# Down slots of three dense feed forwards as three single-pass products, their remainders on GpSimd

## The chip, the cores and the metric

One NeuronCore of a Trainium2 chip runs the kernel. The metric is the device time of one execution in microseconds.

## What is computed

Two two-layer blocks behind each other on a sequence of 256 tokens of width 1024, batch 1, all float32. The plan of four layers is `first0`, `first1`, `even`, `odd`. Each layer is a mixer, an output product and a feed forward, each with a norm and a modulation. Three of the four feed forwards are dense; `first1` has a mixture of 8 experts. Cut to what matters:

```python
def swiglu(x, w1, w3, w2):                       # first0
    return (jax.nn.silu(x @ w1) * (x @ w3)) @ w2

def conv_ffn(h, w_up, conv_w, conv_b, w_down):   # even, odd
    gate, val = jnp.split(h @ w_up, 2, axis=-1)
    gate = causal_dwconv(gate, conv_w) + conv_b  # 3 taps
    return (jax.nn.silu(gate) * val) @ w_down

mod = cond @ w_ada[layer] + b_ada[layer]         # 6 x 1024 numbers for each layer
```

with `D_FF = 2816`. The change touches the dense products with `w2` and `w_down`.

## The kernel before

Weights stream from HBM in slots of 128 x 2048 floats (1 MB) through a ring of six (`ring`, RING = 6), loaded by SP in the order in which TensorE uses them; a place in the ring is loaded anew when the semaphore `weights_used` says that the slot six places earlier has been used. A dense feed forward is 11 chunks of 256 hidden columns. A chunk c has three slots: two for up (w = 0 and 1) and one for down. TensorE's order is up(0), then up(c+1), down(c) for c = 0 to 9, then down(10). Chunks 0, 1 and 10 are written out, 2 to 9 are a loop of two chunks per turn (`each_chunk`); the other engines call `visit(c, odd)` in the same order.

A product can be made in two ways. `mm` on float32 data takes four passes. The other way (`mm3`) takes a number apart into a part rounded to float32r and the remainder, and sums three products of a single pass: high x high, high x low and low x high. The up slots of chunks 1 to 10 are made so: ACT copies the slot from `ring` to one of four buffers `w_high` (`high`, L1095), which rounds it; GpSimd subtracts this from the slot in place (`low`, L732), which leaves the remainder in `ring_rounded`, the same memory; TensorE waits for it on `split_low`. In the same way `h_high` (L1099) and `h_low` (L725) are made once per feed forward. up(0) and all down slots are made with four passes, straight from `ring` and from `ff_hid`.

For chunk c ACT's visit is: the loads of a group of modulation weights (below), rounding of up(c+1), w = 0 (`high(c, odd, 0)`), silu of both halves of chunk c (L1134, or L1128 after the convolution), rounding of up(c+1), w = 1. DVE's visit: in `even` and `odd` the convolution from PSUM into `ff_mid` (L1805, L1808), then two products with silu into `ff_hid` (L1802), and, for chunks 2 to 9 of `first0` and `even`, a group of the next layer's modulation (`mod_parts`): three slots of 128 x 2048, each in two dots of 1024 columns (`dot`, L1814, SCALAR_TENSOR_TENSOR with an accumulator). ACT loads the three slots of a group (L813) only when `mod_part` counts all dots of the group before. `odd` is the last layer and has no such dots. GpSimd has nothing else in these stretches than L725 and L732.

```python
load_modulation(n + 1, c - 2)          # ACT: waits mod_part of the group before
...
pool.wait_ge(split_high, q + (before + 1))   # GpSimd, L731
pool.tensor_tensor(ring_r[:, at, :], ring[:, at, :], f32(w_high[r]), ALU.subtract)
```

## Time and profile before

| | us |
|---|---|
| median of 3 runs | 2631.04 (2624.57 to 2635.58) |
| the profiled execution's own time | 2632.19 |
| its span, first to last instruction | 2630.4 |
| PE busy | 2494.7 (95%) |
| DVE busy | 1773.1 (67%) |
| ACT busy | 1199.3 (46%) |
| POOL busy | 332.0 (13%) |

PE is TensorE, PEld its weight loads, DVE VectorE, ACT ScalarE, POOL GpSimd. A row of a timeline gives the start in us from the start of the span, the duration, the engine, the line and the instruction, output<-inputs, how many are merged (x3), and in brackets the idle time before with what ended it. An instruction that waits for a memory port counts as busy. A matmul in four passes stands as two records, and ends of matmuls are modelled.

### The profile page before, as it was taken

To read this page: it belongs to the slowest core of one execution; us is meant where nothing else is said; L and a number is where in the kernel's file an instruction comes from. 1 tells how busy PE (TensorE), PEld (TensorE's weight loads), DVE (VectorE), ACT (ScalarE), POOL (GpSimd) and SP (SyncE) were. 2 spreads that over 40 slices of the span, in tenths; PEclk is the share of its full clock that TensorE was granted. 3 is DMA by queue.
4 is the path that set the end of the run, shared out by engine and by line. 5 is a ranking of instruction groups with operands and counts; after the bars stand their busy time and mean duration, and the time that the engine had idled before them with its cause. 6 is when DMAs were issued, how large, how long until landed. Compare 5 with 4: busy or idle time off the path is not lost.

```text
span 2630.4 us, 36293 instructions
## 1 busy us (share of the span) xinstructions
PE 2494.7 (95%) x13972; PEld 2157.5 (82%) x13972; DVE 1773.1 (67%) x1949; ACT 1199.3 (46%) x1273; POOL 332.0 (13%) x97
## 2 busy tenths in 40 slices
PE   4999999989999999999999998899999899988999
PEld 3888997877888888888888886788999788977998
DVE  5832775768888888888888886374389777751222
ACT  3213213117676767666666665222321456642221
POOL 0005541000000000000000000010455000001542
PEclk8989999999999999999999999899999999988999
DMA  8845874766999999999999998121588343322542
GB/s 343 320 150 208 347 317 168 288 240 257 349 336 343 342 340 341 342 342 342 340 343 340 341 343 318 65 96 65 202 335 321 124 145 131 142 96 80 172 165 95
DMA packets 90380, 656.13 MB, mean 249 GB/s; under 512 B 10032, under 2 KB 10288, under 8 KB 10800
## 3 DMA queue, kind: packets, MB, share of 16 engines
q1 hardware_dynamic: 80928, 589.34, 59.9%
q10 hardware_dynamic: 9360, 65.52, 6.2%
q8 instruction: 64, 1.05, 0.2%
q14 instruction: 28, 0.23, 0.0%
HBM read 653.76 MB, written 1.05 MB: 249 GB/s over the span
## 4 chain that ended last, share of the span: by engine, by line
PE 71%; issue 17%; POOL 6%; DVE 2%; ACT 2%; DMA 2%; ACTq 0%; POOLq 0%; DVEq 0%
PE bank L1158 70%; POOL ring_rounded L732 6%; DMA consts<-consts_dram 1%; PE bank L1663 1%; DVE rstd L1862 0%; ACT ff_mid L1060 0%; DVE xT L1808 0%; DMA ring<-stream_dram 0%; ACT ff_silu L1059 0%; ACT work_rounded L773 0%; PE bank L1514 0%; DVE work L1808 0%; DVE work L2375 0%; DVE yT L1808 0%; DVE ring L1814 0%
## 5 line engine op out<-in xcount | busy, mean ns | idle before, releaser
L1802 DVE TENSOR_TENSOR ring_rounded<-ring,work_rounded 128x2048 fp32r<-128x2048 f32 x372 | 842.2, 2290 | 142.0 <-ACT work_rounded L907 121.7
L1158 PE MATMUL bank<-work_rounded,proj_rounded 128*128 128x512 f32 x1792 | 614.2, 406 | 2.4 <-DVE proj_rounded L1802 2.0
L907 ACT ACTIVATE work_rounded<-ring 128x2048 fp32r<-128x2048 f32 x224 | 428.3, 1913 | 0.0
L1158 PEld LDWEIGHTS bank<-work_rounded,proj_rounded 128*128 128x128 f32 x1792 | 338.0, 189 | 78.7 <-issue 3.0
L1158 PE MATMUL bank<-ring_rounded,proj_rounded 128*128 128x512 f32 x896 | 353.4, 394 | 0.0
L1158 PE MATMUL bank<-work_rounded,ff_hid_rounded 128*128 128x512 f32 x896 | 302.2, 398 | 1.8 <-DVE ff_hid_rounded L1802 1.8
L1158 PE MATMUL bank<-yT_rounded,ring_rounded 128*128 128x256 f32 x960 | 271.6, 283 | 0.0
L1158 PE MATMUL bank<-hT,ring 128*128 128x256 f32 x1088 | 250.7, 392 | 10.4 <-ACT hT L797 10.4
L1158 PEld LDWEIGHTS bank<-hT,ring 128*128 128x128 f32 x1088 | 213.3, 197 | 48.9 <-issue 18.8
L1158 PE MATMUL bank<-ff_hid,ring 128*128 128x256 f32 x1056 | 232.9, 379 | 0.0
L1158 PEld LDWEIGHTS bank<-ff_hid,ring 128*128 128x128 f32 x1056 | 198.4, 190 | 25.9
L914 ACT ACTIVATE work_rounded<-ring 128x2048 fp32r<-128x2048 f32 x112 | 214.2, 1913 | 0.0
L1158 PEld LDWEIGHTS bank<-work_rounded,ff_hid_rounded 128*128 128x128 f32 x896 | 170.2, 190 | 42.8 <-DVE ring_rounded L1802 2.0
L1158 PEld LDWEIGHTS bank<-ring_rounded,proj_rounded 128*128 128x128 f32 x896 | 170.5, 190 | 36.6
L1158 PEld LDWEIGHTS bank<-yT_rounded,ring_rounded 128*128 128x128 f32 x960 | 184.1, 192 | 0.0
L1158 PE MATMUL bank<-ring_rounded,ff_hid_rounded 128*128 128x512 f32 x448 | 178.6, 399 | 0.0
L705 POOL COPY ff_hid<-proj 128x4 f32<-128x4 f32 (+1 forms) x2 | 0.7, 363 | 1286.5 <-ACT proj L820 1286.5
L732 POOL TENSOR_TENSOR ring_rounded<-ring,proj_rounded 128x2048 fp32r<-128x2048 f32 x30 | 144.4, 4823 | 135.4 <-ACT proj_rounded L1095 135.4
L930 ACT ACTIVATE ff_hid_rounded<-bank 128x256 fp32r<-128x256 f32 x112 | 43.1, 385 | 254.4 <-PE bank L1663 243.0
L732 POOL TENSOR_TENSOR ring_rounded<-ring,work_rounded 128x2048 fp32r<-128x2048 f32 x30 | 143.4, 4794 | 114.6 <-ACT work_rounded L1095 114.6
L1805 DVE TENSOR_SCALAR ff_mid<-bank,params 128x256 f32<-128x256 f32 x44 | 23.9, 543 | 194.5 <-PE bank L1158 194.5
L1158 PE MATMUL bank<-yT_rounded,proj_rounded 128*128 128x256 f32 x480 | 138.2, 288 | 2.6 <-POOL ring_rounded L732 2.6
(286 smaller groups left out, 4264.5 us busy)
## 6 DMA issues: line engine op xcount, KB each, us to landing
ring<-stream_dram SPq DMA_DIRECT2D x561, 1024.0 KB, 4.8
work<-stream_dram ACTq DMA_DIRECT2D x56, 1024.0 KB, 9.2
params<-params_dram ACTq DMA_DIRECT2D x1, 1728.5 KB, 28.9
consts<-consts_dram ACTq DMA_DIRECT2D x1, 1568.0 KB, 37.7
cond<-cond_dram ACTq DMA_DIRECT2D x2, 512.0 KB, 3.8
xT<-x_dram ACTq DMA_DIRECT2D x1, 1024.0 KB, 10.0
out_dram<-xT SPq DMA_DIRECT2D x1, 1024.0 KB, 3.9
consts<-consts_dram ACTq DMA_DIRECT2D x1, 577.0 KB, 32.3
```

What stands on the lines that cost most here:

```text
L705: pool.tensor_copy(d[:, j:4, 0:lag], src[:, j:4, 0:lag])
L732: pool.tensor_tensor(ring_r[:, at, :], ring[:, at, :], f32(w_high[r]), ALU.subtract)\
L907: act.activation(up_high[u][half], ring[:, (moe_first + s + half) % RING, :], ACT.Copy)\
L914: act.activation(down_high[u], ring[:, (moe_first + s) % RING, :], ACT.Copy)\
L930: act.activation(ff_hid_r[:, u, :], bank(4 + u, 0, T), ACT.Copy).then_inc(m["hid_t"], 1)
L1158: return pe.matmul(o, lhsT=a, rhs=b, start=start, stop=stop, skip_group_check=True)
L1663: last = pe.transpose(bank(4 + u, j * P, j * P + P), ff_mid[:, u, j * P:j * P + P], const("ident"))
L1802: return dve.tensor_tensor(o, a, b, op)
L1805: return dve.tensor_scalar(o, a, s1, s2, op0, op1)
```

## The change

The third slot of a chunk is now taken apart like the first two.

- ACT: at the end of a visit it waits for `ffn_hid` of the chunk, copies both halves of `ff_hid` to `ff_hid_high` (128 x 512, rounded), and rounds the down slot of the chunk into one of two buffers `ff_down_high`. For the last chunk this is the only rounding of the visit.
- GpSimd: 31 remainders for each dense feed forward instead of 20; a loop turn has six, one more stands behind the loop.
- DVE: a subtraction (`leave_low`, 128 x 512) leaves `ff_hid_low`. In chunks with modulation it stands behind the first of the three slots.
- TensorE: down(c) is 48 products of one pass instead of 16 in four, and waits for `split_low` and `hid_low`.
- `ff_hid_high` and `ff_hid_low` lie in `h_heads`; `cond` is moved behind it, so that the rounded names keep the same addresses as the plain ones. Before the mixer of `first1` GpSimd's memsets now wait until the first feed forward is done, since its buffers lie in the same memory.

```diff
--- before.py
+++ after.py
@@ -198,12 +198,12 @@
         proj = sb("proj", shapes["proj"])
         ff_hid = sb("ff_hid", shapes["ff_hid"])
         work = sb("work", shapes["work"])
-        cond = sb("cond", [P, D])
         ring_r, yT_r, ff_hid_r, work_r = (rounded[name] for name in ("ring", "yT", "ff_hid", "work"))
         pflat = proj[:, :, :, :].rearrange("p a b t -> p (a b t)")
         pflat_r = rounded["proj"][:, :, :, :].rearrange("p a b t -> p (a b t)")
         hT = sb("hT", shapes["hT"])
         h_heads = sb("h_heads", shapes["h_heads"])
+        cond = sb("cond", [P, D])
         xT = sb("xT", [P, KD, T])
         consts = sb("consts", [P, const_n])
         params = sb("params", [P, param_n])
@@ -364,7 +364,10 @@
         w_high = [work_r[:, 0:SLOT], work_r[:, SLOT:2 * SLOT], pflat_r[:, 0:SLOT], pflat_r[:, 2 * SLOT:3 * SLOT]]
         h_high = yT_r
         h_low = pflat_r[:, SLOT:2 * SLOT].rearrange("p (k t) -> p k t", k=KD)
-        assert mod_at >= 2 * SLOT
+        ff_down_high = [work_r[:, mod_at + (MOD_GROUP + u) * SLOT:mod_at + (MOD_GROUP + 1 + u) * SLOT] for u in range(2)]
+        assert mod_at >= 2 * SLOT and mod_at + (MOD_GROUP + 2) * SLOT <= work_n - D
+        ff_hid_high, ff_hid_low = (rounded["h_heads"][:, a * 4 * T:(a + 1) * 4 * T].rearrange("p (b t) -> p b t", b=4)
+                                   for a in range(2))
 
 
         weights_here = [sem(f"weights_here{i}") for i in range(RING)]
@@ -391,6 +394,7 @@
         low_pool = steps("low_pool", "h")
         split_high = sem("split_high")
         split_low = sem("split_low")
+        hid_high, hid_low = sem("hid_high"), sem("hid_low")
         ffn_mid = sem("ffn_mid")
         ffn_silu = sem("ffn_silu")
         ffn_hid = sem("ffn_hid")
@@ -488,8 +492,9 @@
             return ap.bitcast(F32)
 
 
-        SPLITS = 2 * (DENSE_CHUNKS - 1)
-        PAIR_SPLITS = 4
+        SPLITS = 3 * (DENSE_CHUNKS - 1) + 1
+        PAIR_SPLITS = 6
+        split_buffers = [w_high[0], w_high[1], ff_down_high[0], w_high[2], w_high[3], ff_down_high[1]]
         dense_before = [sum(k != "first1" for k in plan[:n]) for n in range(len(plan))]
 
         def each_chunk(eng, chunks, visit):
@@ -677,6 +682,8 @@
 
                 if n:
                     pool.wait_ge(mod_part, parts_before(n + 1))
+                    pool.wait_ge(weights_used, place[f"in{n}"])
+                    pool.wait_ge(split_low, dense_before[n] * SPLITS)
                 else:
                     pool.wait_ge(mod_part, KD)
 
@@ -725,16 +732,17 @@
                 pool.tensor_tensor(h_low, hT[:, :, :], f32(h_high[:, :, :]), ALU.subtract)\
                     .then_inc(*low_pool.step("h"))
 
-                def low(r, q):
-
-                    at = (first + r // 2 * 3 + r % 2) % RING
+                def low(r, q, high):
+
+                    at = (first + r) % RING
                     pool.wait_ge(split_high, q + (before + 1))
-                    pool.tensor_tensor(ring_r[:, at, :], ring[:, at, :], f32(w_high[r]), ALU.subtract)\
+                    pool.tensor_tensor(ring_r[:, at, :], ring[:, at, :], f32(high), ALU.subtract)\
                         .then_inc(split_low, 1)
 
                 with pool.Fori(0, SPLITS // PAIR_SPLITS) as i:
                     for r in range(PAIR_SPLITS):
-                        low(r, i * PAIR_SPLITS + r)
+                        low(r, i * PAIR_SPLITS + r, split_buffers[r])
+                low(0, SPLITS - 1, ff_down_high[0])
 
             for n, kind in enumerate(plan):
                 if kind.startswith("first"):
@@ -1081,9 +1089,9 @@
             def feed_forward(n, kind):
                 base, first = tiles_before[n], place[f"ffn{n}"]
 
-                def high(c, odd, w):
-
-                    at = 3 * odd + w + 2
+                def high(c, odd, w, final=False):
+
+                    at = 3 * odd + (0 if final else w) + 2
                     rounds = (first + at) // RING + 1
                     if isinstance(c, int):
                         act.wait_ge(weights_here[(first + at) % RING], 16 * (rounds + (c - odd) // 2))
@@ -1092,7 +1100,7 @@
                     else:
                         act.wait_ge(weights_here[(first + at) % RING], (c - odd) * 8 + 16 * rounds)
                         act.wait_ge(weights_used, c * 3 + (first + w - 3))
-                    act.activation(w_high[2 * odd + w], ring[:, (first + at) % RING, :], ACT.Copy)\
+                    act.activation(split_buffers[3 * odd + w], ring[:, (first + at) % RING, :], ACT.Copy)\
                        .then_inc(split_high, 1)
 
                 act.wait_ge(*shift_act.at("h7", 2 * n + 1))
@@ -1114,6 +1122,12 @@
                     tiles(c, odd)
                     if not (isinstance(c, int) and c == 0) and not final:
                         high(c, odd, 1)
+                    act.wait_ge(ffn_hid, base + 2 * c + 2)
+                    if not isinstance(c, int) or c >= 2:
+                        act.wait_ge(weights_used, c * 3 + (first - 1))
+                    act.activation(ff_hid_high[:, 2 * odd:2 * odd + 2, :], ff_hid[:, 2 * odd:2 * odd + 2, :], ACT.Copy)\
+                       .then_inc(hid_high, 1)
+                    high(c, odd, 2, final)
                     if n == 0 and final:
                         condition(cond[:, :])
 
@@ -1708,9 +1722,10 @@
 
                 def split_here(c, w, i):
 
-                    q = splits + 2 * (c - 1) + w + 1
+                    r = 3 * (c - 1) + w
+                    q = splits + r + 1
                     pe.wait_ge(split_low, q if i is None else i * PAIR_SPLITS + q)
-                    return w_high[2 * ((c - 1) % 2) + w], ring_r[:, (first + 3 * c - 1 + w) % RING, :]
+                    return split_buffers[r % PAIR_SPLITS], ring_r[:, (first + 2 + r) % RING, :]
 
                 def mm3(o, w, x, start, stop):
 
@@ -1747,18 +1762,20 @@
                         last.then_inc(weights_used, 1)
 
                 def down(c, i=None, final=False):
-                    at = ff_down(first, c, chunks)
-                    arrive(at, i)
-                    w2 = down_k(at)
-                    t = base + 2 * c + 2
-                    pe.wait_ge(ffn_hid, t if i is None else i * 4 + t)
+                    r = SPLITS - 1 if final else 3 * c + 2
+                    q = splits + r + 1
+                    pe.wait_ge(split_low, q if i is None else i * PAIR_SPLITS + q)
+                    parts = [p.rearrange("p (j n) -> p j n", j=2)
+                             for p in (ff_down_high[c % 2], ring_r[:, (first + 2 + r) % RING, :])]
+                    t = dense_before[n] * DENSE_CHUNKS + c + 1
+                    pe.wait_ge(hid_low, t if i is None else i * 2 + t)
                     for j in range(2):
                         b = 2 * (c % 2) + j
                         for d in range(KD):
 
-                            last = mm(bank(d // 2, d % 2 * T, d % 2 * T + T), w2[:, j, d * P:d * P + P],
-                                      ff_hid[:, b, :], i is None and c == 0 and j == 0 and d % 2 == 0,
-                                      final and j == 1)
+                            last = mm3(bank(d // 2, d % 2 * T, d % 2 * T + T), [p[:, j, d * P:d * P + P] for p in parts],
+                                       (ff_hid_high[:, b, :], ff_hid_low[:, b, :]),
+                                       i is None and c == 0 and j == 0 and d % 2 == 0, final and j == 1)
                             if final and j == 1 and d in (1, 3, 5):
                                 last.then_inc(ffn_out, 1)
                     last.then_inc(weights_used, 1)
@@ -2443,14 +2460,24 @@
                                     last.then_inc(ffn_mid, 1)
                             if back < 2:
                                 last.then_inc(ffn_conv, 1)
+                    def leave_low():
+                        dve.wait_ge(hid_high, c + (dense_before[n] * DENSE_CHUNKS + 1))
+                        tt(ff_hid_low[:, 2 * odd:2 * odd + 2, :], ff_hid[:, 2 * odd:2 * odd + 2, :],
+                           f32(ff_hid_high[:, 2 * odd:2 * odd + 2, :]), ALU.subtract).then_inc(hid_low, 1)
+
                     for j in range(2):
                         b = 2 * odd + j
                         dve.wait_ge(ffn_silu, base + 2 * c + j + 1)
                         if late:
                             dve.wait_ge(weights_used, first + 3 * c - 1)
+                            dve.wait_ge(hid_low, c + (dense_before[n] * DENSE_CHUNKS - 1))
                         tt(ff_hid[:, b, :], bank(4 + b, T, 2 * T), ff_silu[:, b, :], ALU.mult).then_inc(ffn_hid, 1)
                     if n + 1 < len(plan) and not isinstance(c, int):
-                        mod_parts(n + 1, c - 2, range(MOD_GROUP))
+                        mod_parts(n + 1, c - 2, range(1))
+                        leave_low()
+                        mod_parts(n + 1, c - 2, range(1, MOD_GROUP))
+                    else:
+                        leave_low()
 
                 each_chunk(dve, chunks, visit)
                 g = mod_columns(n, 5)
```

On GpSimd, the loop of the feed forward of `first0`. Before, one turn and what follows it (L732 is a remainder, L683 the first memset of the next mixer):

```order
L735 ISA
L732 TENSOR_TENSOR ring_rounded<-ring,work_rounded 128x2048 [waits split_high]
L731 REGISTER_ALU
L732 TENSOR_TENSOR ring_rounded<-ring,work_rounded 128x2048 [waits split_high]
L731 REGISTER_ALU
L732 TENSOR_TENSOR ring_rounded<-ring,proj_rounded 128x2048 [waits split_high]
L731 REGISTER_ALU
L732 TENSOR_TENSOR ring_rounded<-ring,proj_rounded 128x2048 [waits split_high]
L735 REGISTER_ALU
L735 COMPARE_AND_BRANCH
L683 MEMSET work 128x1024 [waits mod_part]
```

Now, from the third remainder of a turn on:

```order
L739 TENSOR_TENSOR ring_rounded<-ring,work_rounded 128x2048 [waits split_high]
L738 REGISTER_ALU
L739 TENSOR_TENSOR ring_rounded<-ring,proj_rounded 128x2048 [waits split_high]
L738 REGISTER_ALU
L739 TENSOR_TENSOR ring_rounded<-ring,proj_rounded 128x2048 [waits split_high]
L738 REGISTER_ALU
L739 TENSOR_TENSOR ring_rounded<-ring,work_rounded 128x2048 [waits split_high]
L742 REGISTER_ALU
L742 COMPARE_AND_BRANCH
L739 TENSOR_TENSOR ring_rounded<-ring,work_rounded 128x2048 [waits split_high]
L690 MEMSET work 128x1024 [waits split_low,weights_used,mod_part]
```

A turn of two chunks has six remainders where it had four, the third and the sixth for down slots; a last one stands in front of the memset, whose waits have become three.

On DVE, in a visit of the loop of `first0`, before (L1802 is the product with silu, L1814 the dots):

```order
L1802 TENSOR_TENSOR ff_hid<-bank,ff_silu 128x256 [waits weights_used,ffn_silu]
L1830 ISA
L1814 ISA [waits mod_here0]
L1814 SCALAR_TENSOR_TENSOR work,mod<-work,cond 128x1024
L1814 ISA
L1814 SCALAR_TENSOR_TENSOR work,mod<-work,cond 128x1024
L1814 ISA [waits mod_here1]
L1814 SCALAR_TENSOR_TENSOR work,mod<-work,cond 128x1024
L1814 ISA
```

Now:

```order
L1819 TENSOR_TENSOR ff_hid<-bank,ff_silu 128x256 [waits hid_low,weights_used,ffn_silu]
L1847 ISA
L1831 ISA [waits mod_here0]
L1831 SCALAR_TENSOR_TENSOR work,mod<-work,cond 128x1024
L1831 ISA
L1831 SCALAR_TENSOR_TENSOR work,mod<-work,cond 128x1024
L2464 REGISTER_ALU
L1819 TENSOR_TENSOR h_heads_rounded<-ff_hid,h_heads_rounded 128x512 [waits hid_high]
L1831 ISA [waits mod_here1]
L1831 SCALAR_TENSOR_TENSOR work,mod<-work,cond 128x1024
```

Behind the second dot there is a subtraction that waits for ACT's copy (`hid_high`); four dots stand behind it.

On ACT, the end of a visit of the loop, now (L1148 is silu, L1103 a rounding, L1128 the copy of `ff_hid`); before, it ended with the rounding of up:

```order
L1148 ACTIVATE ff_silu<-bank 128x256 [waits weights_used]
L1102 REGISTER_ALU [waits weights_here5]
L1103 ACTIVATE work_rounded<-ring 128x2048 [waits weights_used]
L1125 REGISTER_ALU
L1127 REGISTER_ALU [waits ffn_hid]
L1128 ACTIVATE h_heads_rounded<-ff_hid 128x512 [waits weights_used]
L1101 REGISTER_ALU
L1103 ACTIVATE work_rounded<-ring 128x2048 [waits weights_used,weights_here0]
```

The copy and the rounding of the down slot are behind everything else of the visit, and in front of the next group's loads.

## Rows read from the trace of the kernel before

**Rows 1.** The page, busy time of the engines.
```profile
PE 2494.7 (95%) x13972; PEld 2157.5 (82%) x13972; DVE 1773.1 (67%) x1949; ACT 1199.3 (46%) x1273; POOL 332.0 (13%) x97
```

**Rows 2.** Table of windows: busy us of PE, PEld, DVE, ACT, POOL; clock, DMA.
```profile
203.00:409.00 206.00, 204.36 (x1371) 192.56 (x1370) 117.58 (x126) 51.10 (x54) 104.86 (x24) 1.00 0.74 288
1842.00:2056.00 214.00, 209.74 (x1379) 196.26 (x1380) 153.52 (x199) 54.59 (x59) 102.96 (x21) 0.98 0.71 277
2418.00:2625.00 207.00, 206.68 (x1376) 195.22 (x1376) 44.45 (x101) 51.05 (x52) 96.11 (x21) 0.99 0.39 137
```

**Rows 3.** Timeline of POOL in `first0` and `odd`: start, us, instruction, idle before.
```profile
359.61 10.09 POOL L732 TENSOR_TENSOR ring_rounded<-ring,work_rounded 128x2048 fp32r<-128x2048 f32 x2 [9.40 <-ACT work_rounded L1095]
...
2524.45 4.60 POOL L732 TENSOR_TENSOR ring_rounded<-ring,proj_rounded 128x2048 fp32r<-128x2048 f32 x1 [9.13 <-ACT proj_rounded L1095]
```

**Rows 4.** Timeline of ACT in the same visit of `first0`.
```profile
356.06 1.37 ACTq L813 DMA_DIRECT2D work<-stream_dram  x3
357.62 1.91 ACT L1095 ACTIVATE work_rounded<-ring 128x2048 fp32r<-128x2048 f32 x1 [15.25 <-issue]
359.44 0.64 ACT L1134 ACTIVATE ff_silu<-bank 128x256 f32<-128x256 f32 x2
```

**Rows 5.** Timeline of DVE in the same visit.
```profile
359.94 0.76 DVE L1802 TENSOR_TENSOR ff_hid<-bank,ff_silu 128x256 f32<-128x256 f32 x2 [4.06 <-ACT ff_silu L1134]
361.13 4.09 DVE L1814 SCALAR_TENSOR_TENSOR work<-work,cond 128x1024 f32<-128x1024 f32 x1 [0.43 <-DMA work<-stream_dram]
...
365.15 5.63 DVE L1814 SCALAR_TENSOR_TENSOR work<-work,cond 128x1024 f32<-128x1024 f32 x1
...
370.71 1.22 DVE L1814 SCALAR_TENSOR_TENSOR work<-work,cond 128x1024 f32<-128x1024 f32 x1
...
374.14 1.22 DVE L1814 SCALAR_TENSOR_TENSOR work<-work,cond 128x1024 f32<-128x1024 f32 x1
```

**Rows 6.** Timelines of POOL (visits 3, 9) and PE (norm after) in `first0`, `even`.
```profile
261.49 4.58 POOL L732 TENSOR_TENSOR ring_rounded<-ring,proj_rounded 128x2048 fp32r<-128x2048 f32 x1 [8.27 <-ACT proj_rounded L1095]
...
379.11 10.09 POOL L732 TENSOR_TENSOR ring_rounded<-ring,proj_rounded 128x2048 fp32r<-128x2048 f32 x2 [9.41 <-ACT proj_rounded L1095]
...
409.13 3.62 PE L1158 MATMUL bank<-hT,consts 128*128 128x256 f32 x16
...
1908.43 4.55 POOL L732 TENSOR_TENSOR ring_rounded<-ring,proj_rounded 128x2048 fp32r<-128x2048 f32 x1 [8.18 <-ACT proj_rounded L1095]
...
2025.52 10.09 POOL L732 TENSOR_TENSOR ring_rounded<-ring,proj_rounded 128x2048 fp32r<-128x2048 f32 x2 [9.35 <-ACT proj_rounded L1095]
...
2055.55 3.62 PE L1158 MATMUL bank<-hT,consts 128*128 128x256 f32 x16
```

**Rows 7.** Timeline of PE at the end of `odd`.
```profile
2599.49 0.47 PE L1158 MATMUL bank<-yT_rounded,proj_rounded 128*128 128x256 f32 x1
...
2611.19 13.98 PE L1158 MATMUL bank<-ff_hid,ring 128*128 128x256 f32 x64
```

**Rows 8.** Timeline of ACT in `even`.
```profile
1862.52 1.04 ACT L807 ACTIVATE work<-work 128x1024 f32<-128x1024 f32 x1
```

**Rows 9.** DVE, 128x512, both operands in SBUF: beside POOL's tensor_tensor, and alone.
```profile
1751.34 1.85 DVE L1802 TENSOR_TENSOR work<-work 128x512 f32<-128x512 f32 x1
...
L1802 DVE TENSOR_TENSOR work<-proj x1: 692/692/692, 134.7 to 134.7; 128x512 f32<-128x512 f32 x1
```

**Rows 10.** Timeline of DVE after the last up pair of `odd`.
```profile
2611.39 0.54 DVE L1805 TENSOR_SCALAR ff_mid<-bank,params 128x256 f32<-128x256 f32 x1 [2.33 <-PE bank L1158]
...
2613.91 0.82 DVE L1802 TENSOR_TENSOR ff_hid<-bank,ff_silu 128x256 f32<-128x256 f32 x2 [0.15 <-ACT ff_silu L1128]
```

**Rows 11.** Table of windows, around gaps of PE; the clock is the number after POOL's.
```profile
1839.40:1842.70 3.30, 0.00 (x0) 0.00 (x0) 2.87 (x4) 0.89 (x3) 0.00 (x0) 0.88 0.19 79
1842.70:1849.50 6.80, 6.75 (x18) 5.43 (x19) 2.13 (x6) 6.77 (x10) 2.08 (x1) 0.56 0.26 78
...
1666.00:1674.00 8.00, 8.00 (x34) 7.64 (x34) 2.12 (x9) 4.37 (x10) 0.00 (x0) 0.50 0.00 0
```

## The prediction

> **What bounds the kernel now.** I read the page first, then the three dense feed forwards in a table of windows, then the timelines of each engine inside them. On the page TensorE is busy 95% of the span [rows 1], which would make every product removed from it a gain. The windows say the same of the three stretches that the change touches, each about 206 to 214 us [rows 2]. They mislead in two of the three. In the first and the third dense stretch (layers `first0` and `even`) DVE is busy 118 and 154 us, in the last (`odd`) only 44: there the dots for the next layer's modulation are missing. I call one call of `visit(c, odd)` on an engine a visit.
>
> The timeline of one visit of `first0` shows a ring that closes through four engines. ACT rounds the first up slot of the next chunk (ends at 359.5), and GpSimd starts its remainder at 359.61 [rows 3, 4]. DVE has its two products with silu done by 360.70, and its first dot starts at 361.13, yet takes 4.09 us; the second takes 5.63; the four after it start 1.14 us apart from 370.71 on, and the last, at 374.14, ends at 375.36 [rows 5]. GpSimd's two remainders take 10.09 us together, where two alone take twice 4.6 [rows 3]. The reader is to see an alternation: a dot waits for the end of a whole remainder, then the next remainder waits for one dot of 1.1. Only when the last dot is done does ACT issue the next three modulation loads (here at 356.06 after the dots of the visit before), round (357.62, 1.91) and let GpSimd go on [rows 4]. From one first remainder to the next this makes 4.55 + 1.1 + 4.55 + 1.1 + four dots of 1.14 + 1.5 of loads + 1.9 of rounding = 19.3 us; over six visits it is 19.60 (261.49 to 379.11) and 19.52 (1908.43 to 2025.52) [rows 6]. TensorE needs less, 11.7 + 6.9 = 18.6 a visit, worked out next. So in `first0` and `even` the ring is the bound, and in `odd` TensorE is.
>
> **TensorE's part.** 96 single-pass products of an up pair lie between 2599.49 and 2611.19, 11.70 us or 0.122 each; one down slot in 16 four-pass products takes 6.9 (half of 13.98, less a tail of some 0.15) [rows 7]. Afterwards it is 48 single-pass products: 48 x 0.122 = 5.85, 1.06 us less for each of 33 down slots. The Trainium skill (TensorE: Matmul & The Clock Gate, section "Wait — 56ns, not 53.3ns?") has consecutive warm matmuls apart by their columns at 2.4 GHz plus some 2.5 ns, for these 256 columns 0.109 us; by that page a down slot would take 5.2, and `odd` would gain 7 us more. The row decides, and I use 0.122.
>
> **What is added to the ring, `first0` and `even`.** Per visit there is one more remainder, 4.55 us, as two of them take where no dot is in the way (4.58 and 4.55) [rows 6]. Is it on the ring? ACT's third rounding is ready early: after the first rounding come silu 0.6, second rounding 1.9, the copy of ff_hid 0.6 (half of the 1.04 for 1024 columns) [rows 8], third rounding 1.9, so about 5.0 us after the first remainder's start. The second remainder and the second dot end only at 11.3. GpSimd is then waiting, takes its turn, and DVE's next instruction is blocked until 15.9. That next instruction is the new subtraction of ff_hid, 128x512 with two SBUF operands; alone it takes 0.69 [rows 9]. Both come before the four remaining dots, so the ring grows by 4.55 + 0.69 = 5.2, to 24.7. That the subtraction waits for GpSimd at all I take from the row at 1751.34: the same shape, 1.85 instead of 0.69 while GpSimd runs a tensor_tensor [rows 9]. The Trainium skill (SBUF: State Buffer, "Who interferes with whom") says that a DVE instruction with two SBUF inputs and a GpSimd one that reads SBUF exclude each other for a whole instruction. If the row and the rule did not hold for it, the subtraction would slip in beside GpSimd and the ring would be 0.7 shorter, 10 us in all.
>
> Six intervals from visit 3 to visit 9 give 6 x 5.2 = 31.2 us per stretch. Visit 2 runs the first ring of that kind, but starts after down(0), 1.06 shorter: +4.1. TensorE's gain in down slots is worth nothing here: it has 11.7 + 5.85 = 17.6 of work in 24.7 and idles 7.
>
> **The end of each stretch** is new. Before, the last down slot needed no GpSimd. Now its rounding comes after the copy of ff_hid, and its remainder after that. Counting from the first remainder of visit 9 in `first0`: dots done at 15.75 + 5.2 = 20.95, silu and product 1.5, copy 0.6, rounding 1.9, remainder 4.55, products 5.85: 35.4, against 30.0 now (379.11 to the next norm at 409.13) [rows 6]; +5.4. In `even` the convolution comes between, 3.5 us from the end of up to the last ff_hid and some 0.6 for the pair's first step behind the dots [rows 10]: 38.0 against 30.0; +8.0.
>
> Sum of `first0`: 4.1 + 31.2 + 5.4 = +40.7. Of `even`: 4.1 + 31.2 + 8.0 = +43.3.
>
> **`odd`** has no dots. GpSimd's three remainders of 4.6 and the subtraction, 14.5, fit into TensorE's 17.6. The tightest one is the second up slot: silu done 3.0 after the end of up, rounding 1.9, remainder 4.6, ready at 9.5 and needed at 11.7. So nine down slots save 9 x 1.06 = 9.5. At the end, from the end of the last up (2611.19): ff_hid at 3.5 [rows 10], copy, rounding, remainder to 10.6, products to 16.4, against 13.8 now: +2.6. Net -6.9.
>
> **The clock at restarts.** After TensorE had done nothing from 1839.40 to 1842.70, the granted clock was 0.56 for 6.8 us, mostly its 1.2 GHz level, then 1.00 [rows 11]: a loss of 0.44 x 6.8 = 3.0. In front of the last down slot TensorE now idles about 4 to 7 us in all three stretches. Bounds are 0 and 3.0 each; I take 2.5, since the idle is at least as long as in that row: +7.5. Inside the visits the same restart costs nothing: up(c+1) ends at 4.6 + 11.7 + 3.0 = 19.3, before the dots do at 20.95.
>
> **At nothing:** the new waits of GpSimd before its memsets (they move from behind the dots to behind the last down slot; 3 us of work that DVE first needs after norm and the first slots of `first1`), the wait of DVE on hid_low (it is two visits old), the moved `cond`. Loads rise in no place: the same megabytes in a longer visit.
>
> **Sum:** 40.7 + 43.3 - 6.9 + 7.5 = +84.6 on the profiled execution's 2632.19: 2717. The median of the runs shown is 1.2 lower, so 2716.
>
> **Rivals.**
> *Dots and remainders do not exclude each other once three are queued, TensorE bounds all three stretches.* This ends on the other side. Each stretch saves 11 x 1.06 = 11.7 and pays a stall of about 4.9 at its end, and `first0` and `even` save at most the 1.6 and 4.3 us in which TensorE now waits in them [rows 2]: 3 x -6.8 - 5.9 = -26, 2605. It decides from the point where a dot beside a remainder takes under 2 us. Against it stand 4.09 and 5.63 in rows 5; for it only that TensorE looks full in rows 2. 4%.
> *The third remainder falls behind the dots.* If ACT's third rounding came later than 11.3 after the first remainder, GpSimd would do it beside loads and rounding (3.4 us), where nothing on DVE waits. The ring grows by about 0.7 alone; 14 x 0.7 + ends 13.4 - 6.9 + 7.5 = +24, 2656. It has 6 us of room, so 5%.
> *The clock stays low.* With a gap in every visit TensorE might stay at 1.2 GHz for the whole of it: 144 products at up to twice 0.122 are 35.1, over 24.7, +10.4 in 16 visits: up to 2880. For it: at 1666 to 1674, between chains with gaps, the clock was 0.50 throughout [rows 11]. Against: after the gap at 1842.7 it came back in 6.8 us of dense work, and here 17.6 follow each gap. The Trainium skill (same TensorE page, "HAM oscillation — how this bites in real kernels") tells of a kernel whose every tile starts cold because a wait precedes it; by that rule each visit here starts slow, which by the row is 3.0 us and hidden. 4%.
> The forecast itself has 87%.
>
> **Numbers.** Within the forecast, the subtraction unblocked gives 2706, no clock loss 2709, 1 us more per visit from waits between ACT and GpSimd 2730. Range 2690 to 2745. A measurement of this kernel can tell 0.5% (13 us) from no change. Faster 5%, within 2%, slower 93%.
>
> **What would show it.** In the first and third stretch: first remainders 24.7 apart, three remainders over 15.9 us, three DVE instructions of 4 to 5.6 beside them, the subtraction among them; four dots of 1.2 behind; TensorE idle some 7 of 24.7 with a clock below 1. In `odd`: visits of 17.6 with TensorE unbroken, and a gap of 4.9 before the last down slot. It is wrong if the distance stays under 21, or if DVE's dots beside GpSimd take 1.2.

## The result, and the profile after

| | before | after |
|---|---|---|
| median, us | 2630.85 of 4 runs (2624.57 to 2635.58) | 2712.30 of 4 runs (2704.60 to 2715.96) |
| ratio | 1 | 1.0307 [1.0276, 1.0338] |
| profiled execution, us | 2632.19, span 2630.4 | 2704.60, span 2702.8 |

The kernel is slower by 3.1%, 81 us by the medians. The profiled execution of after is the fastest of its four, so the two traces differ by 72.4 us of span only; the sums below are made against that difference.

First the page of the kernel after, its row of busy times and its chain by engine; the last row is the chain of the kernel before.

```profile
PE 2481.2 (92%) x14500; PEld 2171.4 (80%) x14500; DVE 1911.2 (71%) x1982; ACT 1275.7 (47%) x1339; POOL 504.7 (19%) x130
...
PE 60%; issue 19%; DVE 8%; DMA 6%; POOL 5%; ACT 1%; ACTq 1%; DVEq 0%; POOLq 0%; SPq 0%
...
PE 71%; issue 17%; POOL 6%; DVE 2%; ACT 2%; DMA 2%; ACTq 0%; POOLq 0%; DVEq 0%
```

TensorE is busy 13.5 us less and the span is 72 us more. DVE has 138 us more of busy time, though the added subtractions are only 33 instructions of 0.69 us each when alone (23 us together); the rest is time in which it stands blocked and counts as busy. GpSimd has 173 us more, for 33 remainders of 4.55 (150) and their blocking. In the chain that ended last, TensorE's share fell from 71% before to 60%, and DVE's rose from 2% to 8%.

The three dense stretches in a table of windows (busy time of PE, PEld, DVE, ACT, POOL, then clock, DMA share and GB/s), to be read against [rows 2].

```profile
203.00:449.00 246.00, 205.99 (x1543) 202.76 (x1543) 166.93 (x135) 75.48 (x73) 161.56 (x32) 0.91 0.63 241
1879.00:2134.00 255.00, 209.82 (x1549) 206.46 (x1550) 197.75 (x208) 78.51 (x78) 161.16 (x32) 0.89 0.60 233
2496.00:2697.00 201.00, 195.77 (x1551) 193.42 (x1552) 87.65 (x111) 77.02 (x74) 150.84 (x32) 0.97 0.40 141
```

In `first0` and `even` TensorE has hardly more than 200 us of work in stretches that are now 40 us longer, and its clock is down at 0.9 because it goes idle in every visit. In `odd` the stretch is shorter. One visit of `first0`, the one whose remainders start at 363.76, shows why. The timeline of POOL has its three remainders (second and third row), and beside them the first remainder of visit 3 (265.08), that of visit 9 (412.85) and the stretch's last one (437.78).

```profile
265.08 4.58 POOL L739 TENSOR_TENSOR ring_rounded<-ring,proj_rounded 128x2048 fp32r<-128x2048 f32 x1 [8.19 <-ACT proj_rounded L1103]
...
363.76 10.03 POOL L739 TENSOR_TENSOR ring_rounded<-ring,proj_rounded 128x2048 fp32r<-128x2048 f32 x2 [8.78 <-ACT proj_rounded L1103]
373.75 5.60 POOL L739 TENSOR_TENSOR ring_rounded<-ring,work_rounded 128x2048 fp32r<-128x2048 f32 x1
...
412.85 10.04 POOL L739 TENSOR_TENSOR ring_rounded<-ring,proj_rounded 128x2048 fp32r<-128x2048 f32 x2 [9.05 <-ACT proj_rounded L1103]
...
437.78 4.50 POOL L739 TENSOR_TENSOR ring_rounded<-ring,work_rounded 128x2048 fp32r<-128x2048 f32 x1 [9.33 <-ACT work_rounded L1103]
```

The timeline of ACT in the visit at 363.76 and at the start of the next.

```profile
361.77 1.92 ACT L1103 ACTIVATE proj_rounded<-ring 128x2048 fp32r<-128x2048 f32 x1 [17.79 <-issue]
...
365.92 0.63 ACT L1128 ACTIVATE h_heads_rounded<-ff_hid 128x512 fp32r<-128x512 f32 x1
366.44 1.91 ACT L1103 ACTIVATE work_rounded<-ring 128x2048 fp32r<-128x2048 f32 x1
384.65 1.36 ACTq L821 DMA_DIRECT2D work<-stream_dram  x3
386.21 1.92 ACT L1103 ACTIVATE work_rounded<-ring 128x2048 fp32r<-128x2048 f32 x1 [17.87 <-issue]
```

And the timeline of DVE in the same visit.

```profile
366.67 2.70 DVE L1831 SCALAR_TENSOR_TENSOR work<-work,cond 128x1024 f32<-128x1024 f32 x1 [1.75 <-DMA work<-stream_dram]
...
369.30 5.58 DVE L1831 SCALAR_TENSOR_TENSOR work<-work,cond 128x1024 f32<-128x1024 f32 x1
...
374.81 5.09 DVE L1819 TENSOR_TENSOR h_heads_rounded<-ff_hid,h_heads_rounded 128x512 fp32r<-128x512 f32 x1
379.82 1.21 DVE L1831 SCALAR_TENSOR_TENSOR work<-work,cond 128x1024 f32<-128x1024 f32 x1
...
383.26 1.21 DVE L1831 SCALAR_TENSOR_TENSOR work<-work,cond 128x1024 f32<-128x1024 f32 x1
```

The three remainders end at 379.35, 15.6 after the first began. ACT's third rounding of the visit, that of the down slot, was done at 368.35, 5.4 us before GpSimd got to it, so it was never late. The three DVE instructions beside the remainders end at 369.3, 374.8 and 379.8: each ends about when a remainder and its own short turn are over. The third is the subtraction of `ff_hid`, 5.09 us for what takes 0.69 alone. Only then come the four remaining dots (1.15 apart), ACT's loads and the next rounding. In this visit the next first remainder starts at 388.21, 24.45 later.

For `even` the first remainders of visits 3 and 9 and the next norm; then `odd`, whose loop has no dots: the first and the last remainder of a visit, the subtraction, and TensorE's first products of an up pair, of its down slot, and of the next up pair.

```profile
1947.60 10.02 POOL L739 TENSOR_TENSOR ring_rounded<-ring,proj_rounded 128x2048 fp32r<-128x2048 f32 x2 [8.60 <-ACT proj_rounded L1103]
...
2094.83 10.04 POOL L739 TENSOR_TENSOR ring_rounded<-ring,proj_rounded 128x2048 fp32r<-128x2048 f32 x2 [8.78 <-ACT proj_rounded L1103]
...
2134.42 1.89 PE L1172 MATMUL bank<-hT,consts 128*128 128x256 f32 x8
...
2597.61 4.63 POOL L739 TENSOR_TENSOR ring_rounded<-ring,proj_rounded 128x2048 fp32r<-128x2048 f32 x1 [2.95 <-ACT proj_rounded L1103]
...
2614.79 9.66 POOL L739 TENSOR_TENSOR ring_rounded<-ring,work_rounded 128x2048 fp32r<-128x2048 f32 x2 [2.94 <-ACT work_rounded L1103]
...
2615.26 4.71 DVE L1819 TENSOR_TENSOR h_heads_rounded<-ff_hid,h_heads_rounded 128x512 fp32r<-128x512 f32 x1 [1.78 <-ACT h_heads_rounded L1128]
...
2649.46 0.28 PE L1172 MATMUL bank<-yT_rounded,work_rounded 128*128 128x256 f32 x1
...
2660.96 0.40 PE L1172 MATMUL bank<-h_heads_rounded,work_rounded 128*128 128x256 f32 x2
...
2666.64 0.28 PE L1172 MATMUL bank<-yT_rounded,proj_rounded 128*128 128x256 f32 x1
...
2688.77 0.79 PE L1172 MATMUL bank<-h_heads_rounded,work_rounded 128*128 128x256 f32 x2 [4.79 <-POOL ring_rounded L739]
```

Visits of `odd` are 17.18 apart on both engines. The subtraction is blocked there too (4.71), but nothing waits for it. The last row is the gap before the last down slot.

Each stretch from its first single-pass product to the next layer's norm (for `odd`, to the end of its last down slot), read from the timeline of PE of each kernel's profiled execution, is the measure for everything that follows. "Rest" is the span without the three; it lies between 2042.2 and 2050.0 in the nine traces, with no order by kernel, so a single execution carries up to 8 us of chance.

| us | first0 | even | odd | sum | rest |
|---|---|---|---|---|---|
| before | 193.6 | 196.1 | 191.5 | 581.2 | 2049.2 |
| after | 234.2 | 240.0 | 185.5 | 659.8 | 2043.0 |
| e1, third remainder behind the dots | 205.8 | 211.2 | 184.4 | 601.3 | 2050.0 |
| e2, subtraction behind the dots | 227.8 | 236.2 | 184.4 | 648.4 | 2042.2 |
| e3, third remainder narrow | 196.1 | 201.2 | 178.8 | 576.2 | 2045.5 |
| e4, last down slot in four passes | 228.8 | 232.0 | 179.1 | 639.8 | 2044.7 |
| e5, the change in `odd` alone | 193.8 | 196.2 | 179.1 | 569.1 | 2048.1 |
| e6, dots of `even` with one operand | 234.5 | 189.0 | 185.5 | 608.9 | 2047.4 |
| e7, all work kept, down slots in four passes | 236.7 | 242.3 | 198.2 | 677.2 | 2048.2 |

So against before the three stretches of after took +40.6, +43.9 and -5.9, +78.5 together, and the rest -6.2.

### The profile page after: what moved, and what is told of

Read it like the earlier page. It is cut to its first block, busy times and chain, and to the rows that moved or that the text cites. A ratio compares the mean times of both kernels' runs of the same rounds, so it can differ in the third digit from the quotient of the medians.

```text
span 2702.8 us, 37666 instructions
## 1 busy us (share of the span) xinstructions
PE 2481.2 (92%) x14500; PEld 2171.4 (80%) x14500; DVE 1911.2 (71%) x1982; ACT 1275.7 (47%) x1339; POOL 504.7 (19%) x130
## 4 chain that ended last, share of the span: by engine, by line
PE 60%; issue 19%; DVE 8%; DMA 6%; POOL 5%; ACT 1%; ACTq 1%; DVEq 0%; POOLq 0%; SPq 0%
PE bank L1172 59%; POOL ring_rounded L739 5%; DVE work L1831 4%; DMA work<-stream_dram 4%; DVE h_heads_rounded L1819 2%; DMA consts<-consts_dram 1%; PE bank L1677 1%; DVE rstd L1879 0%; DMA ring<-stream_dram 0%; ACTq L821 0%; DVE ring L1831 0%; DVE ring_rounded L1819 0%; DVE xT L1825 0%; POOLq L175 0%; ACTq L761 0%
## 5 line engine op out<-in xcount | busy, mean ns | idle before, releaser
L915 ACT ACTIVATE work_rounded<-ring 128x2048 fp32r<-128x2048 f32 x224 | 428.5, 1914 | 0.0
L739 POOL TENSOR_TENSOR ring_rounded<-ring,work_rounded 128x2048 fp32r<-128x2048 f32 x63 | 315.8, 5032 | 106.5 <-ACT work_rounded L1103 106.5
L1172 PE MATMUL bank<-h_heads_rounded,work_rounded 128*128 128x256 f32 x1440 | 303.1, 285 | 17.8 <-POOL ring_rounded L739 17.8
L1172 PE MATMUL bank<-yT_rounded,ring_rounded 128*128 128x256 f32 x960 | 283.4, 295 | 0.0
L1172 PEld LDWEIGHTS bank<-h_heads_rounded,work_rounded 128*128 128x128 f32 x1440 | 240.9, 194 | 21.3 <-POOL ring_rounded L739 18.4
L922 ACT ACTIVATE work_rounded<-ring 128x2048 fp32r<-128x2048 f32 x112 | 214.2, 1912 | 0.0
L1172 PEld LDWEIGHTS bank<-yT_rounded,ring_rounded 128*128 128x128 f32 x960 | 197.0, 205 | 0.0
L1172 PE MATMUL bank<-yT_rounded,proj_rounded 128*128 128x256 f32 x480 | 144.3, 301 | 39.5 <-POOL ring_rounded L739 39.5
L1172 PE MATMUL bank<-yT_rounded,work_rounded 128*128 128x256 f32 x480 | 142.6, 297 | 31.2 <-POOL ring_rounded L739 31.2
L1103 ACT ACTIVATE work_rounded<-ring 128x2048 fp32r<-128x2048 f32 x63 | 118.9, 1901 | 107.9 <-issue 107.9
```

Source lines behind the costliest of these rows:

```text
L739: pool.tensor_tensor(ring_r[:, at, :], ring[:, at, :], f32(high), ALU.subtract)\
L915: act.activation(up_high[u][half], ring[:, (moe_first + s + half) % RING, :], ACT.Copy)\
L922: act.activation(down_high[u], ring[:, (moe_first + s) % RING, :], ACT.Copy)\
L1103: act.activation(split_buffers[3 * odd + w], ring[:, (first + at) % RING, :], ACT.Copy)\
L1172: return pe.matmul(o, lhsT=a, rhs=b, start=start, stop=stop, skip_group_check=True)
```

## The experiments

The theory: the added remainder stands in the alternation of GpSimd and DVE, and takes the added subtraction into it. Rivals: the remainders' number alone costs, wherever they stand; the clock at restarts costs; TensorE's saving is smaller than costed. Medians of before beside e1 to e4 are 2629.84 (13 runs), beside e5 to e7 2628.48 (11 runs), and each ratio below is to the one beside it. Differences to the kernel after are to its median of 2712.30 and carry the 1 to 2.4 us by which these medians of before differ.

### e1: the third remainder waits for the visit's dots

```diff
-                def low(r, q, high):
+                def low(r, q, high, i=None):
                     at = (first + r) % RING
                     pool.wait_ge(split_high, q + (before + 1))
+                    if i is not None and r % 3 == 2 and n + 1 < len(plan):
+                        pool.wait_ge(mod_part, i * (2 * MOD_GROUP) + (parts_before(n + 1) + (r // 3 - 1) * MOD_GROUP))
```

> The changed kernel, but in first0 and even GpSimd takes the third remainder of a visit (the down slot) only when all six dots of that visit are done. The same work on every engine. Theory (shared access of DVE and GpSimd, and the ring through ACT): the third remainder then lies beside ACT's loads and rounding, blocks neither the subtraction nor a dot, and the distance of first remainders falls from 24.6 to 21.2 us (4.55 + 1.1 + 4.55 + 1.1 + 0.6 + 4.6 + 4.55); over seven intervals in each of two stretches -48, about 2664. Rival (the cost is GpSimd's and TensorE's extra work or waits as such, not who blocks whom): down slots come later, so no gain or slower, 2712 or more.

Measured: 2653.76 (2653.16 to 2654.90), ratio 1.0085 [1.0068, 1.0102]: 58.5 us less than after, with the same instructions. Timelines of POOL and DVE in `first0` of this kernel:

```profile
342.18 4.60 POOL L741 TENSOR_TENSOR ring_rounded<-ring,work_rounded 128x2048 fp32r<-128x2048 f32 x1 [6.36 <-DVE work L1833]
346.73 10.19 POOL L741 TENSOR_TENSOR ring_rounded<-ring,proj_rounded 128x2048 fp32r<-128x2048 f32 x2
363.28 4.53 POOL L741 TENSOR_TENSOR ring_rounded<-ring,work_rounded 128x2048 fp32r<-128x2048 f32 x1 [6.36 <-DVE work L1833]
```

```profile
331.29 5.62 DVE L1833 SCALAR_TENSOR_TENSOR work<-work,cond 128x1024 f32<-128x1024 f32 x1
...
336.84 0.68 DVE L1821 TENSOR_TENSOR h_heads_rounded<-ff_hid,h_heads_rounded 128x512 fp32r<-128x512 f32 x1
337.44 1.21 DVE L1833 SCALAR_TENSOR_TENSOR work<-work,cond 128x1024 f32<-128x1024 f32 x1
```

The third remainder starts when the last dot ends (342.18) and runs beside ACT's loads and rounding, where DVE has nothing to do. The subtraction takes 0.68. The ring is 21.10 here (342.18 to 363.28) instead of 24.6. What a remainder costs is decided by where it stands: the same 4.6 us of GpSimd, with the subtraction, adds 5.0 us to a ring of 19.6 in one place and 1.5 in the other. The rival that the number alone counts is out. The gain is larger than the 48 that I expected from seven intervals in each of two stretches. `first0` is 28.4 us shorter: six intervals explain 21.5 of it, the first visits 3.3 (the seventh interval), and the tail from the first remainder of visit 9 on another 3.5, for which I had no term (4.1 in `even`).

### e2: the subtraction behind all six dots

```diff
                     if n + 1 < len(plan) and not isinstance(c, int):
-                        mod_parts(n + 1, c - 2, range(1))
-                        leave_low()
-                        mod_parts(n + 1, c - 2, range(1, MOD_GROUP))
-                    else:
-                        leave_low()
+                        mod_parts(n + 1, c - 2, range(MOD_GROUP))
+                    leave_low()
```

> The changed kernel with DVE's subtraction of ff_hid behind all six dots instead of behind the second. Theory: the third remainder then blocks the third dot instead of the subtraction, and the subtraction's own 0.6 us leave the ring; 24.0 instead of 24.6, -8 in all, about 2704; a dot of 5.6 stands where the subtraction of 5.1 stood. Rival (the place of the subtraction is what delays the dots): the ring falls by 5, about 2640.

Measured: 2700.35 (2692.45 to 2701.80), ratio 1.0262 [1.0245, 1.0280], 12.0 less than after, some 11 by the stretches. Timeline of DVE in `first0`:

```profile
340.51 5.63 DVE L1831 SCALAR_TENSOR_TENSOR work<-work,cond 128x1024 f32<-128x1024 f32 x1
...
346.07 5.63 DVE L1831 SCALAR_TENSOR_TENSOR work<-work,cond 128x1024 f32<-128x1024 f32 x1
...
355.07 0.68 DVE L1819 TENSOR_TENSOR h_heads_rounded<-ff_hid,h_heads_rounded 128x512 fp32r<-128x512 f32 x1
```

A dot has taken the subtraction's place beside the third remainder, and is blocked in the same way (5.63). Three dots follow instead of four, and the subtraction goes behind them, where ACT's loads no longer wait for it: the ring is 23.94 (334.87 to 358.81 on POOL), 0.7 shorter, the subtraction's own length. So the subtraction does not cause the blocking; whatever two-operand instruction is next in DVE's queue stands still for one remainder.

### e3: the third remainder narrow

GpSimd takes 128 of the 2048 columns of the third remainder, and all products with it use these 128. This leaves out the remainder of the rest of each down slot.

```diff
+                    m = P if r in (2, 5, RING) else SLOT
-                    pool.tensor_tensor(ring_r[:, at, :], ring[:, at, :], f32(high), ALU.subtract)\
+                    pool.tensor_tensor(ring_r[:, at, 0:m], ring[:, at, 0:m], f32(high)[:, 0:m], ALU.subtract)\
                         .then_inc(split_low, 1)
...
-                            last = mm3(bank(d // 2, d % 2 * T, d % 2 * T + T), [p[:, j, d * P:d * P + P] for p in parts],
+                            last = mm3(bank(d // 2, d % 2 * T, d % 2 * T + T), [parts[0][:, j, d * P:d * P + P], parts[1][:, 0, 0:P]],
```

> The changed kernel with GpSimd's third remainder cut to 128 of 2048 columns (TensorE's third products all take those 128 columns; the remainder of the rest of a down slot is left out). All semaphores, roundings, the subtraction and TensorE's work stay. Theory: the ring is shorter by a remainder, 24.6 to about 20.4, and the ends by 4.2 each: 2 x 7 x 4.2 + 3 x 4.2 = -71, about 2641. Rival (ACT's added copy and rounding, DVE's subtraction, or TensorE's waits make the loss): little changes, above 2690.

Measured: 2624.26 of 10 runs (2621.66 to 2629.51), ratio 0.9980 [0.9969, 0.9991]. The third remainder on POOL and the subtraction on DVE:

```profile
356.09 1.44 POOL L740 TENSOR_TENSOR ring_rounded<-ring,work_rounded 128x128 fp32r<-128x128 f32 x1
```

```profile
357.14 0.94 DVE L1820 TENSOR_TENSOR h_heads_rounded<-ff_hid,h_heads_rounded 128x512 fp32r<-128x512 f32 x1
```

The last dot before the subtraction still ends at 357.14, and the subtraction is through 0.94 later: the block has shrunk with the remainder. The ring is 20.3 to 20.9, as expected. The total fell by 88 where I expected 71: in front of the last down slots TensorE waits only 0, 1.3 and 0.8 us instead of 5.7, 7.3 and 4.8, and the clock does not fall there, in `odd` too (178.8 against 185.5), which I had not taken into that estimate. All rounding copies, subtractions, waits and products of the change are still in this kernel, and it is back at the time of before (0.2% under it): `first0` and `even` are 2.5 and 5.1 longer than before, `odd` 12.6 shorter. The loss thus hangs on the length of 33 remainders of GpSimd.

### e4: the last of the eleven down slots in four passes

Its rounding, copy, remainder and subtraction are gone, and TensorE takes it from `ring` and `ff_hid` as before.

```diff
-        SPLITS = 3 * (DENSE_CHUNKS - 1) + 1
+        SPLITS = 3 * (DENSE_CHUNKS - 1)
+        HIDS = DENSE_CHUNKS - 1
...
-                low(0, SPLITS - 1, ff_down_high[0])
...
+                    if final:
+                        at = ff_down(first, c, chunks)
+                        arrive(at)
+                        w2 = down_k(at)
+                        pe.wait_ge(ffn_hid, base + 2 * c + 2)
```

> The changed kernel with the last of the 11 down slots of each dense feed forward in four passes as before (30 remainders, no copy and no subtraction in the last visit). Theory: TensorE does down(10) right behind down(9) or as soon as ff_hid is there: -7.5 in first0, -8.5 in even, -6 in odd, about 2690. Rival (the last slot was not late): within 3 us of 2712.

Measured: 2689.02 (2684.39 to 2692.30), ratio 1.0219 [1.0198, 1.0241], 23.3 less than after. Timeline of PE at the end of `odd`; the last single-pass slot began at 2666.58:

```profile
2672.26 7.07 PE L1173 MATMUL bank<-ff_hid,ring 128*128 128x256 f32 x32
```

The last two down slots take 12.75 together, without a gap and at full clock. The stretches are 5.4, 8.0 and 6.5 shorter, where I had expected 7.5, 8.5 and 6. This is what the chain copy, rounding, remainder costs where nothing is left to hide it, restart of the clock included, less the 1.04 us that the slot then loses on TensorE.

### e5: the change in `odd` alone

`first0` and `even` run as before the change. In `odd` the first ten down slots are single-pass and the last is in four passes, as in e4.

```diff
-        SPLITS = 3 * (DENSE_CHUNKS - 1) + 1
-        PAIR_SPLITS = 6
+        HIDS = DENSE_CHUNKS - 1
+        per = [0 if k == "first1" else 3 if k == "odd" else 2 for k in plan]
...
-                    high(c, odd, 2, final)
+                    if not final and per[n] == 3:
...
+                        high(c, odd, 2)
...
-                    r = SPLITS - 1 if final else 3 * c + 2
+                    if final or per[n] == 2:
+                        at = ff_down(first, c, chunks)
```

> The change in the last dense feed forward alone (odd, which has no dots), its last down slot in four passes; first0 and even as before. Theory: ten down slots save 1.06 to 1.24 us each, nothing is paid: -11 to -12 against the kernel before, about 2619. Rival (GpSimd's three remainders slow TensorE even without dots): no gain against before, 2631 or more.

Measured: 2616.18 of 6 runs (2610.84 to 2619.05) against 2628.48, ratio 0.9945 [0.9932, 0.9958]. It beats the kernel before by 12.3 us, 0.5%, and the interval leaves 1 out. The window of `odd` in this kernel:

```profile
2418.00:2617.00 199.00, 193.97 (x1536) 190.72 (x1534) 87.77 (x111) 73.65 (x70) 146.28 (x31) 0.99 0.41 148
```

`odd` takes 179.1 instead of 191.5, and the clock stays at 0.99. GpSimd runs 30 remainders there, ten of them added, without a dot to collide with. So the exchange of four passes for three products pays where TensorE is the bound, by 12.4 us for ten down slots.

### e6: the dots of `even` with one operand

Each dot of `even` is a sum over the same 1024 columns (`one` is set for these dots alone). The product with the condition is left out, so that the modulation of `odd` gets other numbers.

```diff
-            def dot(slot, row, column):
+            def dot(slot, row, column, one=False):
                 for h in range(2):
                     half = slot[:, h * D:h * D + D]
+                    if one:
+                        last = dve.tensor_reduce(column(h), half, AX, ALU.add)
+                        continue
```

> The changed kernel with each of the 48 dots of the even stretch (chunks 2 to 9) replaced by a sum over the same 1024 columns, which reads one operand from SBUF instead of two (the product with the condition is left out there, so the modulation of odd is another). Theory (a DVE instruction with two operands in SBUF and GpSimd's subtraction exclude each other): the sums take some 1.1 us also beside a remainder, only the subtraction still waits, and the even stretch falls from 240 to about TensorE's 17.2 a visit, 185 to 195; about -47 in all, 2665. Rival (any DVE instruction is blocked beside GpSimd): the sums take up to 5.6 as the dots do and the time stays at 2712.

Measured: 2656.46 (2653.80 to 2659.43), ratio 1.0101 [1.0084, 1.0117], 55.8 less than after. Timelines of DVE and POOL in `even`:

```profile
2002.60 2.34 DVE L1832 TENSOR_REDUCE mod<-work 128x1024 f32 x2
2004.86 4.31 DVE L1819 TENSOR_TENSOR h_heads_rounded<-ff_hid,h_heads_rounded 128x512 fp32r<-128x512 f32 x1
2009.09 4.58 DVE L1832 TENSOR_REDUCE mod<-work 128x1024 f32 x4
```

```profile
2003.99 9.66 POOL L739 TENSOR_TENSOR ring_rounded<-ring,work_rounded 128x2048 fp32r<-128x2048 f32 x2 [1.76 <-ACT work_rounded L1103]
```

GpSimd runs from 2003.99 to 2013.65. The last four sums, 1.15 us each, lie wholly beside it and are not held up, and of the first two (2.34 together) the second is under way when it starts. The subtraction between them, with two operands in SBUF, is held up (4.31). With the same remainders, and sums as long as the dots are when nothing is in the way (1.15), `even` falls from 240.0 to 189.0, 7 us below its time before the change, while `first0` stays where it was. This is the alternation by itself: GpSimd's work and DVE's work fit beside each other, and what does not fit is their exclusion. The Trainium skill (SBUF — State Buffer, section "Who interferes with whom") says that tensor_reduce never contends for the shared port and a tensor_tensor with both inputs in SBUF does; by that, the 1.15 and the 4.31 are what is to be seen, and the trace agrees with both.

### e7: everything kept, down slots in four passes

All roundings, remainders and waits stay; TensorE multiplies the rounded part of the slot with the rounded part of `ff_hid` in four-pass products, and the products with remainders are left out.

```diff
-                            last = mm3(bank(d // 2, d % 2 * T, d % 2 * T + T), [p[:, j, d * P:d * P + P] for p in parts],
-                                       (ff_hid_high[:, b, :], ff_hid_low[:, b, :]),
+                            last = mm(bank(d // 2, d % 2 * T, d % 2 * T + T), f32(parts[0])[:, j, d * P:d * P + P],
+                                       f32(ff_hid_high)[:, b, :],
```

> The changed kernel with all its roundings, remainders, subtraction and waits, but TensorE makes the down products in four passes of the rounded parts (the remainders' products are left out). It adds 1.06 to 1.24 us to each of 33 down slots. Theory: in first0 and even this is hidden in TensorE's 6 us of idle time in each visit but the last (two early and the last slot of each show, +1.2 each), in odd all eleven show: +13 in odd, +3 to 4 in each other stretch, about 2732. Rival (TensorE's pace counts in all three): +39, 2751.

Measured: 2727.94 (2725.58 to 2730.91), ratio 1.0376 [1.0360, 1.0393], 15.6 more than after. Two down slots of `odd` on PE:

```profile
2644.26 7.07 PE L1172 MATMUL bank<-h_heads_rounded,work_rounded 128*128 128x256 f32 x32
...
2662.67 7.07 PE L1172 MATMUL bank<-h_heads_rounded,work_rounded 128*128 128x256 f32 x32
```

The visit is 18.41 again, against 17.18: 1.23 us a slot. Of the 17.4 us that the three stretches lose, 12.6 are in `odd` and 2.5 and 2.3 in the other two (I had expected 3 to 4 there). So the products, the purpose of the change, are worth some 16 us in all, and nearly three quarters of it come from the last stretch.

## Why the prediction was right

The forecast of 2716 stands 4 us from the median, and the likeliest case is what happened. That it is so close is in part luck: the working came to +84.6 and the stretches measured +78.5, and the profiled execution, with a rest 6.2 us shorter than that of before, lies 7.7 under the median. Step by step, in the two traces:

| step | predicted | measured |
|---|---|---|
| distance of first remainders, `first0` / `even` | 24.7 | 24.63 / 24.54 |
| six intervals, each stretch | +31.2 | +30.2 / +30.1 |
| up to visit 3 | +4.1 | +3.8 / +4.2 |
| end of `first0`, clock included | +5.4 + 2.5 | +6.6 |
| end of `even`, clock included | +8.0 + 2.5 | +9.6 |
| `odd`, clock included | -6.9 + 2.5 | -5.9 |
| all three | +84.6 | +78.5 |

The measured distances are (412.85 - 265.08) / 6 and (2094.83 - 1947.60) / 6, those of before being in [rows 6]; the ends are 449.46 - 412.85 = 36.6 against 30.0, and 2134.42 - 2094.83 = 39.6 against 30.0.

**The ring.** Both parts of the 5.2 us held; measured it is 5.0. e1 and e3 take the remainder out of the alternation, or nearly so, and the ring falls to 21.1 and about 20.4; e2 takes out the 0.7 of the subtraction and it falls by 0.7. The order that I argued from the rows of before (ACT's rounding early, GpSimd waiting for its turn, DVE's next instruction blocked whatever it is) is that of the trace.

**The ends.** Mechanism right, and without the clock's part (next paragraph) the size is 5.2 in `first0` and 7.2 in `even`, within 1 us of the 5.4 and 8.0 worked out. e4 shows it by itself.

**The clock.** The mechanism held, and I had taken 2.5 for each of three places; they measured 1.4, 2.4 and 2.8. The last down slots of `first0` and `even` and the restart inside a visit, on PE, and two windows of that visit (the clock is the number after POOL's):

```profile
442.33 0.79 PE L1172 MATMUL bank<-h_heads_rounded,work_rounded 128*128 128x256 f32 x2 [5.66 <-POOL ring_rounded L739]
...
2126.33 0.79 PE L1172 MATMUL bank<-h_heads_rounded,work_rounded 128*128 128x256 f32 x2 [7.33 <-POOL ring_rounded L739]
...
368.42 0.58 PE L1172 MATMUL bank<-yT_rounded,proj_rounded 128*128 128x256 f32 x1 [4.41 <-POOL ring_rounded L739]
```

```profile
368.40:373.40 5.00, 4.98 (x23) 4.99 (x24) 5.00 (x3) 0.00 (x0) 5.00 (x1) 0.50 0.88 369
373.40:382.00 8.60, 8.60 (x73) 8.60 (x72) 8.60 (x6) 0.00 (x0) 5.95 (x2) 0.99 0.36 122
```

After a gap of 4.41 the clock was at its 1.2 GHz level for 5 us, and then at 2.4 GHz. The up pair took 14.05 instead of 11.66, 2.4 more, and it was hidden behind the dots as predicted. The last down slots took 7.29 for 5.84 in `first0`, 8.25 in `even` and 8.6 in `odd`. What a restart costs changes from one execution to the next. The last down slot of `odd` waits 4.79 us in the kernel of e1 too, and there took 7.46 instead of 8.6:

```profile
2638.44 0.64 PE L1174 MATMUL bank<-h_heads_rounded,work_rounded 128*128 128x256 f32 x2 [4.79 <-POOL ring_rounded L741]
```

Since the up pairs of `first0` and `even` run slow after each wait, TensorE idles 4.4 to 6.1 us in nearly every visit there, and not the 7 that I gave as a sign.

**TensorE's saving.** I took 1.06 us for a down slot. The change itself measured 1.04, 5.68 (2660.96 to 2666.64) instead of 6.72; but the up pair behind it also takes 11.50 instead of 11.70, because its first product no longer follows a four-pass one: in [rows 7] that first product lasts 0.47, and now 0.28, and in e7, where the down slots have four passes again, the up pair takes 11.70 again. That 0.20 I had put into the price of every single-pass product (0.122; it is 11.50 / 96 = 0.120). Together 1.24 a visit instead of 1.06, which over ten visits is 1.8; less 0.3 for the clock, `odd` gained 1.5 more than costed. The Trainium skill (TensorE: Matmul & The Clock Gate, "Wait — 56ns, not 53.3ns?") would have the products 0.109 apart; the measured 0.120 decides against it here.

**The rivals.** That dots and remainders do not exclude each other is refuted by 5.58 and 5.09 in the timeline of DVE, and e6 shows what it would have given: `even` at 189.0. That the third remainder falls behind the dots did not happen by itself, but e1 made it so, and its 2654 is within 3 us of the 2656 worked out for that case. This agreement is luck: the ring grew by 1.5 and not by 0.7, since the remainder of 4.6 is longer than the loads and the rounding of 3.4 beside it, and the two ends, worked out as 18.4 us longer with their clock, came out 8.5 longer. That the clock stays low is refuted by the window with 0.99.

**The rest.** Outside the three stretches after is 6.2 us shorter in these two traces, for which the prediction had no term. Nearly half of it is one place, the first up slot of `even`, below; and e1, with the same waits outside the stretches, has 2050.0 for its rest. So I take it for the variation between executions, not for the change.

## What to carry to other kernels

Before giving work to an idle engine, ask which other engine it excludes while it runs, and what is next in that engine's queue. GpSimd was busy 13% of the span, yet each added remainder of 4.55 us, with its subtraction of 0.69, cost 5.0 us a visit in two stretches of three: DVE stood still for the whole of it, and the dots that the ring waits for were queued behind. The same work placed where DVE has nothing to do cost 3.5 us less a visit.

Ask of every stretch by itself whether the engine that is relieved is the one that bounds it. TensorE looked 98% busy or more in all three, and only in one of them was a shorter TensorE worth much (e7: 12.6 of 17.4 us); there the change pays (e5), and it pays best with the last slot left as it was (`odd` at 179.1 instead of 185.5), since its preparation has nothing to hide behind.

## What was not expected

**The clock after the same gap.** Before the first up slot of `even` TensorE waits 3.48 us in both kernels. Timeline of PE before:

```profile
1842.75 17.01 PE L1158 MATMUL bank<-hT,ring 128*128 128x256 f32 x64 [3.48 <-ACT hT L797]
```

and after, with the window behind it:

```profile
1880.53 14.05 PE L1172 MATMUL bank<-hT,ring 128*128 128x256 f32 x64 [3.48 <-ACT hT L805]
```

```profile
1880.50:1887.30 6.80, 6.77 (x32) 6.00 (x33) 2.12 (x6) 6.77 (x10) 2.10 (x1) 1.00 0.28 80
```

The same work took 17.01 us at a clock of 0.56 for its first 6.8 us [rows 11] in one execution, and 14.05 at 1.00 in the other. The first up slots of `first0` and `odd` wait 3.48 too, so the nine traces have this gap 27 times. From its first product to the next slot's first, the up slot takes 13.8 to 13.9 us in 6 of them, 15.4 in 13 and 16.4 to 16.7 in 8. In e5 `first0` and `even` run as before the change, and yet the slot of `even` takes 13.8 there and 16.7 before. So this gap costs nothing, 1.5 us or 2.6 to 2.9 us, and from one trace it can't be told which. I had read the row of before, which is one of the dearest, as what such a gap costs. The gaps of 4.4 to 7.3 us in `first0`, `even` and `odd` of the kernel after all had the 1.2 GHz level behind them, and cost 1.4 to 2.8 us.

**The strict turn.** In the visits shown, an engine that was waiting went next, even when the other had its following instruction ready: GpSimd has three remainders queued, and between two of them exactly one DVE instruction passes, of 1.15 or of 0.69. What decides the order was not tried by itself; that never more than one passes is seen in all nine traces, where no remainder queued behind another took over 5.7 us, itself (4.5) and one dot.
